# An RWKV output stage written in another order: early loads, means first, variances for four heads at once

## What is computed

```python
y = rwkv7_scan(... , False) + rwkv7_scan(... , True)      # 8 heads of 64, both directions
mu = jnp.mean(y, axis=-1, keepdims=True)
var = jnp.mean(jnp.square(y - mu), axis=-1, keepdims=True)
y = heads(((y - mu) * lax.rsqrt(var + 64e-5)).reshape(B, T, 512) * ln_w + ln_b)
bonus = jnp.sum(r_h * k_h * r_k, axis=-1, keepdims=True) * v_h
y = (y + bonus).reshape(B, T, 512)
y_rwkv = y * g                                            # g = sigmoid(g_lo) @ g_up
...
y = jnp.concatenate([y_rwkv, y_gla], axis=-1) @ w_out
```

## Time and profile before

| | us |
|---|---|
| median of 3 runs | 3637.83 |
| lowest and highest | 3636.95, 3639.03 |
| the profiled execution | 3642.51 |
| its span | 3641.2 |
| PE, DVE, ACT, POOL busy | 3283.4, 2265.0, 1003.3, 462.9 |

### The profile page before, as it was taken

One profiled execution on the slowest core, in us unless ns is written; L12 is line 12 of the kernel. 1 busy time (PEld: TensorE's weight loads), 2 busy tenths in 40 slices (PEclk: granted clock), 3 DMA queues, 4 the chain that ended last, 5 costly groups with the idle time before them and its releaser, 6 DMA issues.

```text
span 3641.2 us, 56694 instructions
## 1 busy us (share of the span) xinstructions
PE 3283.4 (90%) x24667; PEld 2721.0 (75%) x24667; DVE 2265.0 (62%) x3132; ACT 1003.3 (28%) x1484; POOL 462.9 (13%) x362
## 2 busy tenths in 40 slices
PE   6988799888986899999999888998898899999996
PEld 4777667688884778888888676876776678888885
DVE  5758656677873444444444666996556556666666
ACT  4544234322112221111111352114454211121112
POOL 2520033322222100000000210000001001111110
PEclk9988798999997899999999998999999999999999
DMA  4410054222212111111111212122001111111111
GB/s 133 119 55 14 16 183 125 78 41 41 41 26 102 58 47 52 52 52 52 36 52 41 87 52 65 36 63 67 1 1 58 35 41 47 47 55 49 47 47 64
DMA packets 242719, 207.27 MB, mean 57 GB/s; under 512 B 66744, under 2 KB 205127, under 8 KB 241959
## 3 DMA queue, kind: packets, MB, share of 16 engines
q1 hardware_dynamic: 223527, 176.96, 16.4%
q10 hardware_dynamic: 13824, 25.17, 2.2%
q0 software_dynamic: 5120, 1.53, 0.4%
HBM read 172.06 MB, written 29.64 MB: 55 GB/s over the span
## 4 chain that ended last, share of the span: by engine, by line
PE 70%; DVE 16%; ACT 6%; POOL 3%; DMA 2%; issue 2%; SPq 1%; ACTq 0%; DVEq 0%; POOLq 0%
PE ps L2066 22%; PE ps L2081 16%; PE ps L1929 5%; PE ps L1479 4%; PE ps L641 3%; PE ps L642 3%; PE ps L643 3%; PE ps L2814 2%; DVE Yc L2691 2%; PE ps L2790 2%; POOL a_x L2441 1%; PE ps L2800 1%; DMA s_ZZ<-zd_dram 1%; DVE s_tmp L1662 1%; DVE s_Z L1663 1%
## 5 line engine op out<-in xcount | busy, mean ns | idle before, releaser
L3108 DVE TENSOR_TENSOR H<-H,ps 128x1024 f32<-128x1024 f32 x256 | 312.6, 1221 | 181.5 <-PE ps L2081 174.5
L2231 DVE TENSOR_TENSOR fsum<-fsum,ps 128x1024 f32<-128x1024 f32 x168 | 205.1, 1221 | 311.6 <-PE ps L2081 309.5
L2081 PE MATMUL ps<-dh,hh 128*128 128x512 f32 x864 | 339.7, 393 | 20.6 <-DVE hl L2046 14.7
L2081 PE MATMUL ps<-dl,hh 128*128 128x512 f32 x864 | 338.3, 392 | 0.0
L2081 PE MATMUL ps<-dh,hl 128*128 128x512 f32 x864 | 338.1, 391 | 0.0
L2066 PE MATMUL ps<-hn_h,uh 128*128 128x512 f32 x704 | 275.6, 391 | 7.0 <-DVE ul L1770 4.5
L2066 PE MATMUL ps<-hn_l,uh 128*128 128x512 f32 x704 | 274.8, 390 | 0.0
L2066 PE MATMUL ps<-hn_h,ul 128*128 128x512 f32 x704 | 274.8, 390 | 0.0
L2066 PE MATMUL ps<-hx_h,uh 128*128 128x512 f32 x512 | 201.0, 393 | 8.4 <-DVE hx_l L2046 5.3
L2081 PEld LDWEIGHTS ps<-dh,hh 128*128 128x128 f32 x864 | 163.5, 189 | 58.8 <-DVE hl L2046 16.3
L2066 PE MATMUL ps<-hx_l,uh 128*128 128x512 f32 x512 | 200.4, 391 | 0.0
(11 more groups left out here) (475 smaller groups left out, 7654.9 us busy)
## 6 DMA issues: line engine op xcount, KB each, us to landing
aw<-in_w_ada_dram ACTq DMA_DIRECT2D x96, 256.0 KB, 3.0
uw<-in_w_mlp_dram SPq DMA_DIRECT2D x32, 512.0 KB, 4.2
dw<-in_w_mlp_dram SPq DMA_DIRECT2D x32, 512.0 KB, 5.1
uw<-in_ffn_gate_dram SPq DMA_DIRECT2D x22, 512.0 KB, 3.9
uw<-in_ffn_up_dram SPq DMA_DIRECT2D x22, 512.0 KB, 5.3
dw<-in_ffn_down_dram SPq DMA_DIRECT2D x22, 512.0 KB, 5.9
cw<-in_w_in_dram SPq DMA_DIRECT2D x20, 512.0 KB, 4.0
o_w<-in_w_out_dram SPq DMA_DIRECT2D x16, 512.0 KB, 13.3
```

Source lines behind the costliest of these rows:

```text
L2081: mm = pe.e.matmul(ps[:, 2 * pair + hf, :], v[s][:, blk(t)], w[:, half(hf)], start=(m == 0), stop=(m == 2))
L2231: return dve.c.tensor_tensor(f, f, new, ALU.add) if g else dve.c.tensor_copy(f, new)
L3108: return dve.c.tensor_tensor(h, h, self.ps[:, 4 + 2 * (t % 2):6 + 2 * (t % 2), :], ALU.add)
```

## The change

- **Loads.** The four small loads (`r_hones`, `r_hsel2`, `r_gup`, `r_sglo2`) and `v` are issued in SP's program of the scan, behind its last `inverse_back`. `v` goes into a tile of its own, `r_v`, as `rkv[:, 8:12]` is the place of the scan's values until the scan is over. The meeting of the scan now waits for these loads as well. Behind it are left `y_gla` and `w_out`.
- **The last chunk.** PE leaves out `ss` of chunk 15, and DVE the addition to `S`: nothing reads that state. In its place PE computes `ro_bonus` of 0, in banks 0 and 1. DVE makes all four `ro_rk` in chunk 14.
- **The order in the output stage.** Four pairs of banks are in use (0 and 1, 2 and 3, 4 and 5, 6 and 7) where there were three. The means of 0 and 1 come first, one behind the other, and the later steps of each `c` are laid between those of others, written out by hand on each engine. Bank 6 holds the token sums, which is bank 4 before.
- **Variances** are taken and inverted for two `c` at a time, on 32 columns: twice instead of four times.
- **DVE's last steps** are three instead of four: `ln_w` goes into the product with 1/sqrt(var), `ln_b` into the addition of the bonus, both as SCALAR_TENSOR_TENSOR.
- **ACT and POOL** do the same pieces in another order. In `part`, ACT waits for `ro_bv` of the next `c` besides `ro`.

```diff
+        self.r_sglo2, self.r_gup, self.r_hones = put(116, "r_sglo", [PART, TOK]), put(120, "r_gup", [PART, RW]), put(122, "r_hones", [PART, PART])
+        self.r_hsel2, self.r_v = put(122.5, "r_hsel", [PART, 2]), put(168, "r_v", [PART, 4, TOK])
+        self.r_sq, self.r_wide = [put(at, "r_sq", [PART, TOK]) for at in (124, 128)], [put(at, "r_wide", [PART, TOK]) for at in (112, 136)]
...
         self.inverse_back(sp, self.t_z, NSUB - 1, range(0, 8, 2))
-        self.meet(sp, "rwkv_scan")
+        i = self.i
+        sp.wait_ge(dve["pr", NSUB - 1, 1])
+        for dst, src in ((self.r_hones[:], i["k_head_ones"]), (self.r_hsel2[:], i["k_head_sel"]), (self.r_gup[:], i["rwkv_g_up"][0]),
+                         (self.r_sglo2[:], self.dram["lo"][2])):
+            sp.e.dma_start(dst, src).then_inc(*self.t_misc.one("ro"))
+        sp.e.dma_start(self.r_v[:], self.dram["v"]).then_inc(*self.t_keep.one("v_back"))
...
-            if u >= 0:
+            if u == NSUB - 1:
+                pe.wait_ge(self.t_misc["ro"])
+                self.rwkv_bonus_pe(0, 0)
+                pe.wait_ge(act["U", u, 0], act["U", u, 1])
+            elif u >= 0:
...
-            if u >= 0:
+            if 0 <= u < NSUB - 1:
...
+            if u == NSUB - 2:
+                for c in range(4):
+                    self.rwkv_rk_dve(c)
...
     def rwkv_out_sp(self):
-        sp, i = self.sp, self.i
-        for dst, src in ((self.r_hones[:], i["k_head_ones"]), (self.r_hsel2[:], i["k_head_sel"]), (self.r_gup[:], i["rwkv_g_up"][0]),
-                         (self.r_sglo2[:], self.dram["lo"][2])):
-            sp.e.dma_start(dst, src).then_inc(*self.t_misc.one("ro"))
-        sp.e.dma_start(self.rkv[:, 8:12, :], self.dram["v"]).then_inc(*self.t_keep.one("v_back"))
+        sp = self.sp
         sp.e.dma_start(self.B[:, 4:8, :], self.dram["y_gla"]).then_inc(*self.t_in.one("y_gla_back"))
         self.chunks_sp("o", self.o_w, "w_out")
-        self.meet(sp, "rwkv_out", self.t_misc["ro"], self.t_in["y_gla_back"])
+        self.meet(sp, "rwkv_out", self.t_in["y_gla_back"])
 
...
+    def rwkv_bonus_pe(self, c, base):
+        self.pe.wait_ge(self.dve["ro_rk", c])
+        self.head_sum_pe(self.rkv[:, c, :], base, "ro_bonus", c)
...
+        mean(0, 4)
+        mean(1, 2)
+        pe.wait_ge(dve["ro_bv", 0])
+        self.rwkv_bonus_pe(1, 0)
+        sums(0)
+        pe.wait_ge(dve["ro_y", 0])
+        mean(2, 4)
+        sums(1)
+        pe.wait_ge(dve["ro_y", 1])
+        mean(3, 2)
+        pe.wait_ge(dve["ro_bv", 1])
+        self.rwkv_bonus_pe(2, 0)
+        sums(2)
+        sums(3)
+        pe.wait_ge(dve["ro_y", 2])
+        gate(0, 4)
+        pe.wait_ge(dve["ro_y", 3])
+        over(0, 2)
+        pe.wait_ge(dve["ro_bv", 2])
+        self.rwkv_bonus_pe(3, 0)
+        pe.wait_ge(dve["ro_var", 2])
+        gate(1, 6)
+        pe.wait_ge(dve["ro_m", 0])
+        over(1, 2)
+        pe.wait_ge(dve["ro", 0])
+        gate(2, 4)
+        pe.wait_ge(dve["ro_bv", 3])
+        over(2, 0)
+        pe.wait_ge(dve["ro", 1])
+        gate(3, 6)
+        over(3, 2)
         self.meet(pe, "rwkv_out")
...
+        def part(c):
+            act.wait_ge(dve["ro", c], dve["ro_bv", min(3, c + 1)])
+            self.part_act(self.ys[:, c, :], self.B[:, c, :], "y_h", c)
+
+        square(0)
+        square(1)
+        act.wait_ge(self.t_in["y_gla_back"])
+        for k in (4, 5):
+            self.part_act(self.ys[:, k, :], self.B[:, k, :], "y_h", k)
+        root(0)
+        square(2)
+        wide(0)
+        wide(1)
+        square(3)
+        for k in (6, 7):
+            self.part_act(self.ys[:, k, :], self.B[:, k, :], "y_h", k)
+        root(2)
+        for k in (4, 5):
+            self.chunk_high_act("o", self.o_wh, self.o_w, k)
+        wide(2)
+        for k in (6, 7, 0):
+            self.chunk_high_act("o", self.o_wh, self.o_w, k)
+        wide(3)
+        part(0)
+        self.chunk_high_act("o", self.o_wh, self.o_w, 1)
+        part(1)
+        for k in (2, 3):
+            self.chunk_high_act("o", self.o_wh, self.o_w, k)
+        part(2)
+        part(3)
         self.meet(act, "rwkv_out")
...
-        for kind, k in [("y", 4), ("y", 5), ("y", 6), ("y", 7), ("o", 4), ("o", 5), ("y", 0), ("o", 6), ("o", 7), ("o", 0), ("y", 1), ("o", 1), ("o", 2),
+        for kind, k in [("y", 4), ("y", 5), ("y", 6), ("y", 7), ("o", 4), ("o", 5), ("o", 6), ("o", 7), ("o", 0), ("y", 0), ("o", 1), ("y", 1), ("o", 2),
...
+        def variance(c):
+            dve.wait_ge(pe["ro_sums", c + 1])
+            dve.e.tensor_scalar(self.st[:, 0, 16 * c:16 * c + 32], ps[:, 6, 16 * c:16 * c + 32], 1.0 / 64, 64e-5, ALU.mult, ALU.add) \
+                .then_inc(*dve.one("ro_var", c))
+
+        def inverse(c):
+            x, z, q = (self.st[:, n, 16 * c:16 * c + 32] for n in range(3))
+            dve.wait_ge(act["ro_sqrt", c])
+            dve.c.reciprocal(z, z).then_inc(*dve.one())
+            dve.c.tensor_tensor(q, z, z, ALU.mult).then_inc(*dve.one())
+            dve.c.tensor_tensor(q, q, x, ALU.mult).then_inc(*dve.one())
+            dve.c.tensor_scalar(q, q, -0.5, 1.5, ALU.mult, ALU.add).then_inc(*dve.one())
+            dve.c.tensor_tensor(z, z, q, ALU.mult).then_inc(*dve.one("ro_inv", c))
+
+        def normed(c, base):
+            y = self.B[:, c, :]
+            dve.wait_ge(pe["ro_over", c])
+            dve.c.scalar_tensor_tensor(out=two(y), in0=two(y), scalar=self.col("rwkv_ln_w", c), in1=ps[:, base:base + 2, :], op0=ALU.mult, op1=ALU.mult) \
+                .then_inc(*dve.one("ro_m", c))
+
+        def gated(c, base):
+            y = self.B[:, c, :]
+            dve.c.scalar_tensor_tensor(out=y, in0=y, scalar=self.col("rwkv_ln_b", c), in1=self.rkv[:, 8 + c, :], op0=ALU.add, op1=ALU.add) \
+                .then_inc(*dve.one())
+            dve.wait_ge(pe["ro_gate", c])
+            dve.c.tensor_tensor(two(y), two(y), ps[:, base:base + 2, :], ALU.mult).then_inc(*dve.one("ro", c))
+
+        bonus(0)
+        centre(0, 4)
+        centre(1, 2)
+        bonus(1)
+        centre(2, 4)
+        variance(0)
+        inverse(0)
+        centre(3, 2)
+        bonus(2)
+        variance(2)
+        inverse(2)
+        normed(0, 2)
+        bonus(3)
+        gated(0, 4)
+        normed(1, 2)
+        gated(1, 6)
+        normed(2, 0)
+        gated(2, 4)
+        normed(3, 2)
+        gated(3, 6)
         self.meet(dve, "rwkv_out")
...
```

121 lines of the change are left out of this document (43 added, 78 removed).

## The result

| | before | after |
|---|---|---|
| median, lowest to highest (4 runs each), us | 3638.43, 3636.95 to 3639.43 | 3602.10, 3600.84 to 3603.32 |
| ratio of after to before, 95% interval | | 0.9894, 0.9878 to 0.9909 |
| the profiled execution, us | 3642.51 | 3603.32 |
| its scan's last write to memory (`zd_dram`) | 1083.57 | 1084.79 |
| end of the scan's last addition | 1103.43 | 1106.03 |

The medians differ by 36.3 us, the profiled executions by 39.2. The 39.2 are, in order: +1.2 ahead of the scan's last write, +1.4 from there to the scan's end, -39.4 in the output stage (96.74 to 57.34), -2.4 behind it. So the gain is in the stage. The forecast of 42.5 was 3.3 us too large against the profiled executions and 6.2 against these medians.

The account below looks back on a forecast made before the run. No engine filled the output stage; the turns between engines took the time. POOL starting at 1112.8 plus 37.3, 2.9, 3.2 and 1.5 ended at 1157.7, 42.5 us less: 3637.8 - 42.5 = 3595.3, range 3588 to 3606.

Parts of the forecast that it names:

- the forecast's own case: Output stage: POOL's row sets its end, total 3592 to 3602 us; chance 0.69.
- The third rival: Scan's end: early loads delay the inverse's return, PE gets the last block 7.2 us later, total 3602; chance 0.08.
- Scan's end: Last chunk: dropping ss against a bonus group gains 0.1 us net, DVE's four products overrun by 0.4; ends about 1103.7.
- Loads early: Loads behind the last inverse_back: v lands 10.2 us after issue, at 1099.4, and PE's 5.97 us wait goes.
- The last rival: Output stage: loads come early but the rest is no better, only 5.97 us goes, total 3632; chance 0.02.
- PE starts at once at the high level: Stage's start: PE begins the means without a pause at the high clock, groups about 1.8 us.
- The low clock's rival: Output stage: PE stays at the low clock throughout, saving only 27.9 us, total 3610; chance 0.11.
- y_gla in 8.0 us, POOL from 9.1 us on: Stage's start: y_gla issued at 1103.7 lands at 1111.7; POOL starts at 1112.8, 30.0 us earlier than before.
- POOL bounds the stage: Output stage: POOL ends last; 16 pieces of 2.33 take 37.3 us, plus 2.9 waiting and 3.2 from DVE's additions.
- the waits: POOL's row: its third piece waits 2.9 us for ACT, with DVE's first inversion done at about 1116.4.
- The 1.5 for low clocks: Output stage: PE's partly low clock delays the third part or the end by 0 to 5 us, taken as 1.5.
- DVE's last product at 1147: Stage's end: DVE finishes at 1147, ahead of POOL, which takes that piece at 1153.

Follow-up runs that it names:

- after again: The changed kernel, unchanged, measured a second time on another occasion: median 3609.58 us, ratio to before 0.9900 to 0.9931.
- kernel 1: The changed kernel with its five early loads issued behind the scan's end again: median 3613.51 us, ratio to before 0.9903 to 0.9951.
- kernel 2: The changed kernel with only v's load issued behind the scan's end, ahead of y_gla: median 3615.37 us, ratio to before 0.9910 to 0.9956.
- kernel 5: The kernel before with only the early loads added and v in its own tile: median 3633.79 us, ratio to before 0.9952 to 0.9990.
- kernel 7: The changed kernel with ACT's four y_gla high parts moved behind the fourth square, so POOL starts later: median 3610.03 us, stage 57.51 us.
- kernel 3: The changed kernel with the inversions' small DVE operations given a PSUM operand, one more reciprocal each: median 3601.14 us, stage 53.77 us.

## Why the prediction was right, and where it was off

The forecast was 3595.3, the range 3588 to 3606; the result, 3602.10, lies in it, and the sign is right. On the second occasion after had 3609.58 beside a before of 3643.36, a gain of 33.8: the gain is 34 to 39 us, not 42.5. Of the 6.8 us between forecast and result, 3.3 are the stage (57.3 for 54.0), 1.1 the scan's end, and the other 2.4 or so are spread: +1.2 ahead, -2.4 behind, and 3.5 because before's profiled execution lay 4.7 above its median and after's only 1.2.

The right range has some luck in it. 3602.10 lies just above the span of the forecast's own case (3592 to 3602). The range went on to 3606 for partly low clocks and for loads that hold up the scan, and neither is what took the time. The third rival named 3602 too, by a mechanism that did not occur: the last block of `s_ZZ` came as before. The mechanism of the forecast's case (POOL's row sets the end, with PE at the high level at the start) is what the trace shows.

- *Scan's end* (forecast +0.3; measured +1.4, and +0.5 in after again). Leaving out `ss` gave 1.1 us, not 1.9, and the bonus group cost 1.0, not 1.8 (from the first product of the last chunk's `Rn` group to the scan's end: 6.69 before, 5.59 in kernel 1, 6.63 in after); the net, -0.1, was right. DVE's four products cost the scan nothing (0.4 forecast): `s_T` comes 6.79 us behind the write, 6.77 before. What the sum lacked is PE's gap of 1.11 beside v's load. (Kernel 1's 17.53 from write to scan's end is 1.2 us shorter for another reason: PE was granted 1.00 in the 12 us behind that write, 0.86 before.)
- *Loads early* (right in what it removes, wrong in its price). v comes in 9.8 us after issue, forecast 10.2. PE's 5.97 us are gone, but kernels 1, 2 and 5 put the loads at 10 to 12.5 us of the gain: what the sum lacked is DVE's wait for v (and PE's low level behind it, kernel 2). The last rival, 5.97 alone (3632), is near kernel 5's 3633.79 only by chance: that kernel is 11.0 us below the before of its occasion, and its stage gained 12.5.
- *PE starts at once at the high level* (right): 1.00 granted, groups of 1.84 to 1.96 up to 1125.65, two gates of 3.7. The low clock's rival fell.
- *y_gla in 8.0 us, POOL from 9.1 us on* (right to 0.3 us, and without weight): by kernel 7 the start has 7 us of slack.
- *POOL bounds the stage* (right), and its row: 37.3 for 16 pieces stands; the additions cost it 3.75, forecast 3.2; the waits are 6.9, forecast 2.9. **This term of the sum failed.** It took 2.6 us for two whole inversions and had the first done at "about 1116.4". They ended at 1120.8 and 1134.1, which put 1.8 us onto the wait for the third piece and made the second wait, of 2.17. I had looked for contention only at the wide additions and had not asked it of the narrow operations. With them out of the way (kernel 3) the stage is 53.8, forecast 54.0.
- *The 1.5 for low clocks* had no such use: kernel 3 ends in 53.8 with nearly the same clocks (0.83 in the stage against 0.79). That 53.8 meets 54.0 so closely is luck: its POOL starts 0.3 later than forecast, waits 0.5 more and loses 0.5 more to the additions, and the 1.5 stands in for these.
- *DVE's last product at 1147* (wrong by 10.8 us): 2.3 is the later end of the scan, 8.4 are the two inversions, 3.0 the additions (2.95 where I took 2.20), and against that go the 2 to 3 us of waits for PE that I had put in. DVE's end and POOL's are close again, as before the change, but POOL's last two pieces follow its row without a wait, and the last starts at 1161.0, 2.1 us after ACT has its high part (1158.9).

The trace also says how long one is held. Each of the four additions begins 1.84 to 1.91 us ahead of the end of POOL's running piece and ends 1.08 to 1.09 behind it (it takes 1.28 alone), and POOL's next piece is 1.0 longer for it. The Trainium skill (SBUF — State Buffer, "Who interferes with whom") has this as an exclusive lock, held for the whole instruction, for a DVE instruction with two SBUF inputs against a GpSimd one that reads SBUF. The trace agrees: 2.27 is nearly one piece of 2.33. Had I taken the lock and not a factor of duration from it, every two-input operation beside POOL would have been charged up to 2.33 us, and three of the small ones would have stood out. The fourth, the TENSOR_SCALAR with one input, is not a case of two inputs; it was held all the same (2.26), and the 1.69 of the wide one before could have warned me.

## What to carry to other kernels

Count, beside a busy POOL, the DVE instructions that read two SBUF tensors, and TENSOR_SCALAR from SBUF to SBUF, not their columns: each may wait for the end of one POOL instruction. Here a chain of four tiny ones lost 6.6 us, the four wide additions together 6.7. An operand in PSUM, or a place in the order ahead of POOL's work, takes it away. And when one engine's row is the bound but has waits in it, an earlier start is worth nothing until those waits are gone: ask what ends the last of them.

## What the runs showed of the hardware

- A DVE operation of 32 columns (0.18 to 0.19 us alone) is held to the end of POOL's running instruction, for up to 2.3 us. This was seen for TENSOR_TENSOR with both inputs in SBUF and also for TENSOR_SCALAR with one (2.25 to 2.27; the wide one 0.81 alone, 1.69 to 2.71 beside POOL). It was not for RECIPROCAL (0.35 in both cases), nor for any form here with an operand in PSUM (0.20, and 1.28 and 1.22 for the wide ones). POOL loses nothing to the small ones (its pieces stay at 2.33), and 1.0 to a wide addition.
- PE stands 0.2 to 1.9 us inside a row of products, without a wait in the profile, in nine profiled executions of nine with a 2 MB load under way at that place; with the load moved ahead, the gap moved in one program and was gone in another. Each of these ten gaps ends 1.1 to 1.5 us behind a 16 KB packet of the instruction queue that starts later than in the programs without the load.
- The same program places its scan's last write up to 3.8 us apart in two profiled executions (1084.79 and 1088.55), and up to 16 us apart among kernels that do not differ ahead of it (1077.92 to 1093.89). Gains of under 8 us are found in a stretch of the trace, not in a median.
